# Two blocks of a transformer on one core: the operand buffers of the split matmuls set 64 bytes apart and onto multiples of 64 bytes

## The reference, cut to what matters

```python
def first_block(x, mem, ...):
    proj = _rmsnorm(x, mix_norm_g) @ w_in            # 1024 x 4616
    merged = g_s5 * (y_s5 @ w_br_s5) + g_m * (y_m @ w_br_m)
    x = x + merged @ w_out
    x = x + _cross_attn(_rmsnorm(x, x_norm_g), _rmsnorm(mem, mem_norm_g), x_wq, x_wkv, x_wo)
    u = _causal_dwconv(_rmsnorm(x, f_norm_g) @ w_up, conv_w, conv_b)
    a, b = jnp.split(u, 2, axis=-1)
    x = x + (jax.nn.gelu(a) * b) @ w_down
    return _rmsnorm(x, final_norm_g)

def second_block(x, ...):
    for l in range(2):
        y = even_mixer(x, ...) if l == 0 else odd_mixer(x, ...)
        x = layer_norm(alpha * x + y, ln_g[l, 0], ln_b[l, 0])
        y = conv_ffn(x, ffn_w_up[l], ffn_conv_w[l], ffn_conv_b[l], ffn_w_down[l])
        x = layer_norm(alpha * x + y, ln_g[l, 1], ln_b[l, 1])
    return x
```

## The kernel before, in words

| operand | before | after |
|---|---|---|
| early weights w0 / w1 / w2 / w3 | 96 / 32 / 64 / 32 | 0 / 0 / 0 / 0 |
| early activations yS / yG / yM / M | 64 / 32 / 32 / 32 | 64 / 64 / 64 / 64 |
| late weights `w_parts`, `parts4096` to `parts16384` | 32 | 64 |
| late activations `hT_parts`, `gT_parts` | 32 | 0 |
| `ring`, `memT`, `arena`, `raw`, `arena_late` | 32 | 64 |

## Time and profile before

### The profile page before, as it was taken

How to read it: one execution, slowest core, us unless ns; L and a number is a source line. 1 busy time by engine, 2 the same in 40 slices (tenths; PEclk the granted TensorE clock), 3 DMA queues, 4 the chain that set the end, 5 groups by cost and what they waited for, 6 DMA issues and landing times. The chain is left out here.

```text
span 1275.2 us, 21186 instructions
## 1 busy us (share of the span) xinstructions
PE 1233.4 (97%) x8525; PEld 1137.0 (89%) x8528; DVE 900.8 (71%) x1266; ACT 608.9 (48%) x919; POOL 108.1 (8%) x148
## 2 busy tenths in 40 slices
PE   7999999989999999999998999999999999999997
PEld 5888888979999999899988999998986899999996
DVE  4977996575767888845678666767665589666677
ACT  2242213463655666634664555554423454645552
POOL 2893000003000000010000000000200000000000
PEclk8999999999999999999999999999999799999999
DMA  9544444526725666625334456667355104556560
GB/s 275 168 137 128 132 133 135 191 95 190 235 97 193 207 228 219 211 68 151 111 105 165 151 181 226 198 229 165 101 160 181 35 1 166 191 174 197 183 211 37
DMA packets 178734, 202.76 MB, mean 159 GB/s; under 512 B 21884, under 2 KB 163163, under 8 KB 178636
## 3 DMA queue, kind: packets, MB, share of 16 engines
q1 hardware_dynamic: 175083, 191.49, 47.6%
q0 software_dynamic: 3184, 9.77, 2.5%
q10 hardware_dynamic: 369, 0.13, 0.1%
HBM read 200.30 MB, written 1.08 MB: 158 GB/s over the span
## 5 line engine op out<-in xcount | busy, mean ns | idle before, releaser
L1477 DVE TENSOR_TENSOR w_parts<-raw,w_parts 128x1024 fp32r<-128x1024 f32 (+1 forms) x242 | 294.9, 1218 | 133.8 <-ACT w_parts L1466 128.7
L1760 PEld LDWEIGHTS ps<-hT_parts,w_parts 128*128 128x128 f32 x2880 | 349.1, 192 | 1.9
L1760 PE MATMUL ps<-hT_parts,w_parts 128*128 128x256 f32 x2880 | 350.8, 283 | 0.0
L1466 ACT CAST w_parts<-raw 128x1024 fp32r<-128x1024 f32 (+1 forms) x242 | 252.9, 1045 | 169.3 <-PE ps L1760 70.3
L1779 PE MATMUL ps<-w_parts,gT_parts 128*128 128x512 f32 x720 | 169.5, 391 | 0.8 <-DVE w_parts L1477 0.8
L1779 PEld LDWEIGHTS ps<-w_parts,gT_parts 128*128 128x128 f32 x720 | 133.6, 188 | 28.1 <-DVE w_parts L1477 1.0
L1530 PE MATMUL ps<-hT_parts,w_parts 128*128 128x256 f32 x816 | 101.3, 284 | 2.0 <-DVE w_parts L1477 1.4
L1530 PEld LDWEIGHTS ps<-hT_parts,w_parts 128*128 128x128 f32 x816 | 99.0, 192 | 2.7 <-DVE w_parts L1477 1.7
L477 PE MATMUL ps<-hT,ring 128*128 128x256 f32 x448 | 100.3, 385 | 1.0 <-DVE hT L320 1.0
L477 PEld LDWEIGHTS ps<-hT,ring 128*128 128x128 f32 x448 | 85.7, 193 | 14.2 <-issue 1.6
L1884 DVE SCALAR_TENSOR_TENSOR arena_late<-ps,vecT,arena_late 128x255 f32<-128x255 f32 (+1 forms) x176 | 84.9, 482 | 11.0 <-ACT arena_late L1834 4.7
(11 more groups left out here) (413 smaller groups left out, 1573.3 us busy)
## 6 DMA issues: line engine op xcount, KB each, us to landing
raw<-in_ffn_w_up SPq DMA_DIRECT2D x44, 1024.0 KB, 5.2
raw<-in_f_w_up SPq DMA_DIRECT2D x22, 1024.0 KB, 5.3
raw<-in_ffn_w_down SPq DMA_DIRECT2D x22, 1024.0 KB, 5.0
ring<-in_w_in SPq DMA_DIRECT2D x18, 1024.0 KB, 5.4
raw<-in_ev_w_in SPq DMA_DIRECT2D x15, 1024.0 KB, 5.5
raw<-in_f_w_down SPq DMA_DIRECT2D x11, 1024.0 KB, 4.9
ring<-in_x_wkv SPq DMA_DIRECT2D x8, 1024.0 KB, 5.3
ring<-in_w_out SPq DMA_DIRECT2D x4, 1024.0 KB, 8.3
```

Of the source, the lines that this page charges most:

```text
L1466: self.done(A, A.copy(high[:, c], self.raw[:, u % RAW, c]), self.s_hi)
L1477: self.done(V, V.tensor_tensor(low[:, c], self.raw[:, u % RAW, c], high[:, c].bitcast(F32), ALU.subtract), self.s_lo)
L1760: mm = T.matmul(self.ps[:, b, m * 256:m * 256 + 256], w[:, kk, m * P:(m + 1) * P], x[:, kk, :], start=kk == 0 and q == 0, stop=kk == KD - ...
```

## The change

Buffers are moved; no instruction is added, taken away or put into another place in the order. `pad_line`, 32 bytes behind the constants, moves all that follows to multiples of 64 bytes. `pad_x` and `pad_arena`, 64 bytes each, put `hT_parts` and `gT_parts` 64 bytes off the weights' parts and the arena back. In the early part w1, w2, w3 and yS are moved by 16, 8, 16 and 24 floats, the scratch `sg` by 16, and the scratch `yG` to 12288.

```diff
+LINE = 16
@@ setup_memory
         self.zb = self.sb("zb", [P, 512], BF16)
+        self.sb("pad_line", [P, LINE // 2])
...
-        for name, at, dims in (("w0", 18480, [2, SLOT]), ("w1", 4096, [2, SLOT]), ("w2", 27752, [2, SLOT]), ("w3", 8192, [2, SLOT]), ("yS", 29800, [2, 4, SEQ]),
+        for name, at, dims in (("w0", 18480, [2, SLOT]), ("w1", 4096 + LINE, [2, SLOT]), ("w2", 27760, [2, SLOT]), ("w3", 8192 + LINE, [2, SLOT]), ("yS", 29824, [2, 4, SEQ]),
                                ("yG", 13312, [2, 4, SEQ]), ("yM", 10240, [2, 4, SEQ]), ("M", 0, [2, KD, SEQ])):
@@ block1_memory
-        self.sg, self.yG = p(8192, 4, SEQ), p(9216, 4, SEQ)
+        self.sg, self.yG = p(8192 + LINE, 4, SEQ), p(12288, 4, SEQ)
@@ late_memory
         self.w2p = self.sb("w_parts", [P, 2, 2, SLOT], F32R)
+        self.sb("pad_x", [P, LINE])
         self.hTr = self.sb("hT_parts", [P, 2, KD, SEQ], F32R)[:, :, :, :]
         self.gTr = self.sb("gT_parts", [P, 2, 2, 2, SEQ], F32R)
+        self.sb("pad_arena", [P, LINE])
         self.arena_cols = 26624
```

## The result

The kernel after takes 1267.01 us (median of 5 runs, 1262.96 to 1268.88) beside 1274.55 us for the kernel before (5 runs, 1273.07 to 1276.63). The ratio is 0.993, 95% interval 0.9911 to 0.9949: faster by about 7.5 us. The forecast was 1228 us with a range from 1206 to 1244. The direction was right; the gain is a sixth of the 46 us forecast.

The account below looks back on a forecast made before the run. TensorE, at the pace of its matmuls, was taken to bound the kernel. The matmul terms sum to 50.3 us, less 1.2 for entries and 3 given back: 46 us off 1273.6, so 1228 us, range 1206 to 1244.

Parts of the forecast that it names:

- The bound of 1.2 us for entries: In the sum: each of 146 units has one entry not at the new pace, so 1.2 us less gain.
- The one comparison that decides: Early units 30 and 31, and L615: weights 64 bytes apart from activations give 113.3 ns, same remainder modulo 128 gives 120.0.
- The third rival: All moved operands: 64 bytes act as 32 do, 119 ns, 6 us gained, 1268 us; chance 0.06.
- apart is all that counts: Split matmuls: only distance helps, 113.3 ns and 220.5 ns, 38 us gained, 1235 us; chance 0.25.
- The closing sentence: End of the signs to look for: unequal paces of L1760 and L2173 would show the distance's sign counts; no chance given.
- Part 1: Split matmuls, operands 64 bytes apart: 256 columns from 120.0 to 113.3 ns, 512 from 227.9 to 220.5.
- Part 2: Split matmuls, operands on multiples of 64: 256 columns from 113.3 to 112 ns, 512 from 220.5 to 218.2.
- Deeper: Split matmuls: line start counts fully and weight load shortens, 109.2 and 215.8 ns, 61 us gained, 1213 us; chance 0.17.
- 64 acts as 32: Split matmuls: a 64-byte distance gives the 119 ns of 32 bytes, 6 us gained, 1268 us; chance 0.06.
- No change: Split matmuls: paces have another cause that w0 happens to share, 1274 us; chance 0.07.
- Slower: Split matmuls: the operand leading by a line meets the other again, 3 ns a pair, 18 us lost, 1292 us; chance 0.05.
- all three likely cases: Whole kernel: forecast (1221 to 1232, chance 0.40), apart alone (1232 to 1242, 0.25), deeper (1206 to 1221, 0.17).

Follow-up runs that it names:

- map1: Separate kernel of split-matmul stretches alone, at varied operand starts: 256 columns at 113.3, 117.8 or 120.0 ns; no time for the full kernel.
- g_behind: Kernel after, larger pads: stationary less streaming start +64 bytes for feed-forward's 256 columns, -64 for 512 on `w_parts`; 1258.32 us beside 1275.82, ratio 0.9852.
- line_only: Kernel before with only 32 bytes added behind the constants, late operands on multiples of 64 at distance 0; 1276.71 us beside 1275.0, ratio 1.0013.
- map2: Separate kernel of matmul stretches alone, distances in 16-byte steps and entries without a wait; equal 256-column stretches at +64 took 117.9 or 113.6 ns.
- w_ahead: Kernel after with `hT_parts` and `gT_parts` moved: stationary less streaming start +64 bytes for the feed-forward's 256 and 512 columns; 1265.3 us, ratio 0.9928 to before.
- signed: Kernel after with late buffers moved: stationary less streaming start +64 bytes for the feed-forward's 256 columns, 0 for 512; 1262.42 us, ratio 0.9901 to before.
- map4: Separate kernel of stretches alone, six distances, activations 0, 16 or 8 bytes past a multiple of 32; at -112, 256 columns took 113.3 or 120.0 ns.
- map3: Separate kernel of feed-forward rounds alone, 256- and 512-column stretches without waits, per pair of distances; (+64, -64) held 113.4 ns for 256 columns every round.

## Why the prediction was wrong, step by step

**Right.** That the distance between the stationary and the streaming operand moves the pace, and not the clock, the traffic or the region: map1 has all paces without traffic, and unit 31, moved from D = 0 to +64, went from 120.0 to 113.4 ns. That VectorE's split is indifferent: 1225 ns. That the gain reaches the end: 10.6 us off TensorE are 9.0 off the span, so 1.6 us are given back where I had put 3 (these are two single executions, and the runs of before spread by 3.6 us, those of after by 5.9). The bound of 1.2 us for entries can't be read apart.

**The one comparison that decides: the step that failed.** Unit 30 and L615 on w0 were taken for two witnesses of one case, "64 apart". By D they are two cases, -64 and +64, and the table of places, with its remainder by 128, can't tell them apart. The third rival even names their distances, 192 and 320 bytes; modulo 256 these are -64 and +64. That unit 30 showed the fast one of the two paces of -64 was luck: in after it has the slow one, in g_behind the fast one, at the same addresses. The change gives -64 to L1760 and L1530, 2880 + 816 = 3696 pairs, and to the 660 on `parts`; they settled at 117.8 ns, a gain of 2.2 ns each. The forecast had 8.0, and the rival "apart is all that counts" 6.7. On 4356 pairs the step from 8.0 to 2.2 is 25 us, the largest part of what is missing. The closing sentence named this, a pace of L1760 other than that of L2173 would show that the sign counts; it stood there as a sign to look for and had no chance or price in the forecast. At 117.8 ns for -64 and 113.3 for +64 (L2173 on `w_parts`, L1532 and L1726 on `w_parts`, 396 + 144 + 96 = 636) the late forms would give 4356 x 2.2 + 636 x 6.7 = 13.8 us.

**Part 1, 512 columns.** I gave them the 256-column gain, 6.7 to 7.4 ns, on the reason that the excess belongs to the pair, and I bounded the unseen case by "no gain" although nothing excluded a loss. It is a loss: at D = +64 233.4 instead of 226.7 ns, 792 x 6.7 = 5.3 us by the paces, 4.3 in the rows. The 512-column form has its own best distances, 0 and, where the stationary operand begins on a multiple of 32, -112. This term alone was wrong by 7.7 + 4.3 = 12 us. 13.8 - 5.3 = 8.5 us for the late part; the rows of its forms sum to 8.6.

**Part 2, the lines.** 1.3 ns a pair and 2.3 per 512 columns, some 9 us of the sum: worth nothing. line_only isolates it at a ratio of 1.0013, and map1 shows equal paces on and off a line. That the excess at 113.3 ns equals 16 columns is a coincidence as far as these runs show, and I had built on it.

**The rivals.** "Deeper" falls with the lines; no stretch at any distance went below 113.3 ns with 256 columns. The N/2.4 + 2.5 ns that it rests on is given by the Trainium skill, page "TensorE: Matmul & The Clock Gate", section "Back-to-back issue gap", for the isolated gap of a single matmul, and not for pairs of a weight load and a matmul; the prediction left that out. "64 acts as 32" at 1268 us is nearest in time but wrong in its mechanism: distances of 32 have 116.5 to 118.4 ns, and D = -64 has 117.8 as one of two paces. "No change" had the rule of the Trainium skill on its side, page "TensorE: Matmul & The Clock Gate", section "Part 2: What happens when you issue a matmul", that two independent read ports serve the stream and the weight load. Here the distance of the two operands changes the pace from 113.3 to 120.0 ns with nothing else changed (map1); the measurement decides. That the two reads hinder each other would fit, but no run shows the reads themselves. "Slower" had the right thought, that the one leading by a line differs from the one behind it, but took the sum of both signs as one.

**The range.** It went from 1206 to 1244, since all three likely cases shared the reading that failed. The fast pace had been seen in two runs, of 47 and of 22 matmuls, and was carried over to 5184. The nearest other row, the uneven distance at 119 ns, stood in a rival with a chance of 0.06 at 1268 us; as the upper bound of a pace that no row showed for L1760 it would have kept the time inside the range.

## What to carry to other kernels

Where TensorE is the bound and pairs of one weight load and one matmul follow each other, the starts of the two operands are worth 1.5% of this kernel: give each form of matmul (which operand streams, how many columns) its own measured distance, with its sign and modulo 256 bytes, in a small kernel that holds the real sequence of forms. A pace seen in one run of a trace isn't a property of its addresses until another run with the same signed distance, and another entry, shows it. And an average over a run is a pace only if no long steps lie in it: read the steps from start to start, and set the same run of the kernel before beside it. A buffer moved for one form is at the same time moved for every other form that reads it, so price each of them before the sum.

## What the runs showed of the hardware

- At D = +64 and -64 one and the same sequence of addresses has two lasting paces, 113.3 and 117.8 ns for 256 columns. It falls into one at its start and keeps it. What runs before matters (map2: 5.82 and 5.62 us for equal stretches of 48), but doesn't fix it: the equal early parts of after and g_behind have 117.8 and 113.3 ns in units 28 to 30. In the feed-forward D = -64 had the slow one in 117 of 120 stretches of 24 (after), +64 in 14 (g_behind), 58 (w_ahead) or 104 (signed).
- The distances act modulo 256 bytes: 320 as 64, 192 and 448 as -64, 256 as 0 (map1).
- 512 columns follow another order: 226.7 ns at 0, 228.8 at -64, 233.4 at +64.
- The place within 32 bytes counts as well: at -112, 113.3 or 120.0 ns by which operand carries the 16 bytes (map4), and with 512 columns 226.7 or 233.4 (map2, map3). What in the chip makes these patterns no run here shows.
